# Four small reorderings in a hybrid mLSTM, HGRN2 and attention encoder block on one core

## The reference, cut to what matters

```
z = RMSNorm(x); proj = z @ w_in
y_m = mLSTM branch: 4 heads x 256, chunks of 128, forward and backward
y_h = HGRN2 branch: 8 heads x 128, forward and backward
x = x + (sig(gate_m) * (y_m @ w_branch_m) + sig(gate_h) * (y_h @ w_branch_h)) @ w_out
u = RMSNorm(x, norm_x_g); mn = RMSNorm(mem, norm_mem_g)
probs = softmax((u @ w_q)(mn @ w_k)^T / 16)      # 4 heads x 256, 256 memory tokens
x = x + (probs @ (mn @ w_v)) @ w_o
x = x + ConvGatedFFN(RMSNorm(x)); out = RMSNorm(x)
```

## Time and profile before

| | |
|---|---|
| median of 3 runs | 2550.45 us (2549.9 to 2551.49) |
| profiled execution, its own time | 2551.23 us |
| span of the profiled execution | 2549.5 us |
| mean granted TensorE clock | 0.999 of full speed |
| TensorE busy | 2527.5 us, 99% |
| VectorE busy | 1636.8 us, 64% |
| ScalarE busy | 914.8 us, 36% |
| GpSimd busy | 745.4 us, 29% |

### The profile page before, as it was taken

The page is one execution under the profiler, slowest core; times in us unless marked ns, Lnnn a source line. Parts: engine busy times, 40 slices in busy tenths (PEclk is TensorE's granted clock), DMA queues, the critical chain, the costliest instruction groups (busy, mean ns, idle before and its releaser), DMA issues.

```text
span 2549.5 us, 33564 instructions
## 1 busy us (share of the span) xinstructions
PE 2527.5 (99%) x13158; PEld 2157.2 (85%) x13158; DVE 1636.8 (64%) x1864; ACT 914.8 (36%) x1122; POOL 745.4 (29%) x713
## 2 busy tenths in 40 slices
PE   9999999999999999999999999999999999999998
PEld 9888888889999999997888888876788888888887
DVE  6675555248888888866555424433457998887567
ACT  6342222133333333332323423333333443333433
POOL 2032232002121121234442001177413456553001
PEclk9999999999999999999999999999999999999999
DMA  8323333432223323344443536156414233225755
GB/s 294 121 96 108 99 127 105 140 140 92 84 100 108 107 93 116 108 150 140 165 149 145 201 125 215 34 192 208 155 49 149 85 114 131 101 99 194 276 191 182
DMA packets 181628, 349.67 MB, mean 137 GB/s; under 512 B 10459, under 2 KB 106023, under 8 KB 181472
## 3 DMA queue, kind: packets, MB, share of 16 engines
q1 hardware_dynamic: 119520, 154.44, 18.3%
q0 software_dynamic: 33088, 118.51, 13.3%
q10 hardware_dynamic: 28864, 74.59, 8.0%
HBM read 241.16 MB, written 106.33 MB: 136 GB/s over the span
## 4 chain that ended last, share of the span: by engine, by line
PE 96%; DMA 2%; DVE 1%; ACT 0%; issue 0%; POOL 0%; SPq 0%; ACTq 0%; DVEq 0%; POOLq 0%
PE ps L2301 18%; PE ps L2851 13%; PE ps L2440 12%; PE ps L2869 8%; PE ps L2332 7%; PE ps L2681 7%; PE ps L2507 4%; PE ps L2819 3%; PE ps L2464 3%; PE ps L2590 3%; PE ps L2611 2%; PE ps L2629 2%; PE ps L2379 2%; PE ps L2534 2%; PE ps L2522 1%; PE ps L2792 1%
## 5 line engine op out<-in xcount | busy, mean ns | idle before, releaser
L2301 PE MATMUL ps<-a_hi,whi 128*128 128x512 f32 x576 | 234.2, 407 | 0.0
L2301 PE MATMUL ps<-a_hi,wlo 128*128 128x512 f32 x576 | 224.8, 390 | 0.0
L2301 PE MATMUL ps<-a_lo,whi 128*128 128x512 f32 x576 | 224.4, 390 | 0.0
L1620 DVE TENSOR_TENSOR wlo<-raw,whi 128x2048 fp32r<-128x2048 f32 x59 | 135.8, 2302 | 114.4 <-ACT whi L997 113.3
L997 ACT ACTIVATE whi<-raw 128x2048 fp32r<-128x2048 f32 x59 | 113.1, 1917 | 190.4 <-PE ps L2681 105.1
L1002 ACT ACTIVATE ev<-ps 128x512 f32<-128x512 f32 x128 | 76.6, 599 | 208.0 <-PE ps L2301 131.2
L2332 PE MATMUL ps<-whi,a_hi 128*128 128x256 f32 x512 | 148.1, 289 | 0.0
L2332 PE MATMUL ps<-whi,a_lo 128*128 128x256 f32 x512 | 144.8, 283 | 0.0
L2332 PE MATMUL ps<-wlo,a_hi 128*128 128x256 f32 x512 | 144.7, 283 | 0.0
L793 POOL TENSOR_TENSOR cv<-cv,cs 128x1024 f32<-128x1024 f32 x16 | 38.5, 2404 | 322.6 <-ACT cs L1261 322.6
L2301 PEld LDWEIGHTS ps<-a_hi,wlo 128*128 128x128 f32 x576 | 108.1, 188 | 23.5
(11 more groups left out here) (422 smaller groups left out, 7197.1 us busy)
## 6 DMA issues: line engine op xcount, KB each, us to landing
raw<-in_w_in SPq DMA_DIRECT2D x45, 1024.0 KB, 6.6
raw<-in_w_up SPq DMA_DIRECT2D x22, 1024.0 KB, 5.1
hg_T<-ev ACTq DMA_DIRECT2D x32, 512.0 KB, 3.0
qfb<-hg_T POOLq DMA_DIRECT2D x24, 512.0 KB, 5.5
wd<-in_w_down POOLq DMA_DIRECT2D x44, 256.0 KB, 3.4
down_weight_sums<-wd POOLq DMA_DIRECT2D x22, 512.0 KB, 4.3
hidden_T<-ga ACTq DMA_DIRECT2D x11, 1024.0 KB, 4.0
hidden_sums<-s POOLq DMA_DIRECT2D x10, 1024.0 KB, 4.7
```

The lines of the kernel that those rows point to most:

```text
L1620: signal(dve, dve.tensor_tensor(wlo[:, b.slot], w4[:, b.slot], whi[:, b.slot], ALU.subtract), w_lo, b.count())
L2301: ins = pe.matmul(ps[:, unit_bank(b, u)], W[sw][:, b.slot, k, c * P:(c + 1) * P], op[mw][:, k, t * HALF:(t + 1) * HALF], start=k == 0 and ...
```

## The change

Four edits:

1. SyncE's first loads: the identity and the gain row of the memory norm are issued before the second memory tile, and the first x tile before weight block 1.
2. First mLSTM head (`step` is 0 there): 2 quarters in place of 3 ahead of the scores, one quarter in each of the eight steps (before, none in steps 0, 1 and 7), and after the second head's scores 2 and 1 in place of 3 and 2. The total stays 16.
3. VectorE makes `y_lo` in the iteration of step 6 in place of after step 7.
4. Attention: the reciprocal and multiplication of tile t follow the maximum of tile t, after a wait for its exponential.

```diff
             rows_in(0)
+            sp.dma_start(ident[:], A["c_ident"]).then_inc(id_ld, 16)
+            sp.dma_start(nb["gb"][:, 0], A["norm_mem_g"].to_broadcast([P, D])).then_inc(g_ld, 16)
             rows_in(1)
-            sp.dma_start(nb["gb"][:, 0], A["norm_mem_g"].to_broadcast([P, D])).then_inc(g_ld, 16)
-            sp.dma_start(ident[:], A["c_ident"]).then_inc(id_ld, 16)
             kv_weights(0)
+            rows_in(2)
             kv_weights(1)
-            rows_in(2)
...
+                    if s == 6 and last:
+                        dve.wait_ge(y_cut, 2)
+                        signal(dve, dve.tensor_tensor(y_lo[:], mk[:], y_hi[:], ALU.subtract), y_sub, 2)
                 if not last:
                     head_cols(j + 1)
                     split_lo(b.ahead(1))
-                else:
-                    dve.wait_ge(y_cut, 2)
-                    signal(dve, dve.tensor_tensor(y_lo[:], mk[:], y_hi[:], ALU.subtract), y_sub, 2)
...
-                    if t >= 1:
-                        k = (r - 1) % 3
-                        dve.wait_ge(a_exp, r)
-                        line(dve.reciprocal(mx[:, k, 2:3], mx[:, k, 2:3]))
-                        signal(dve, dve.tensor_scalar(pr[:, k], pr[:, k], mx[:, k, 2:3], None, ALU.mult), a_nrm, r)
+                        dve.wait_ge(a_exp, r + 1)
+                        line(dve.reciprocal(mx[:, r % 3, 2:3], mx[:, r % 3, 2:3]))
+                        signal(dve, dve.tensor_scalar(pr[:, r % 3], pr[:, r % 3], mx[:, r % 3, 2:3], None, ALU.mult), a_nrm, r + 1)
...
                 if not step:
                     ml_keys(0)
-                    quarters(3)
+                    quarters(2)
                     ml_scores(0)
                     quarters(1)
...
                     if s == NT - 1:
-                        quarters(2 if last else 1 if step else 0)
+                        quarters(2 if last else 1)
...
-                        quarters(2 if last else 1 if step or s > 1 else 0)
+                        quarters(2 if last else 1)
                 if not last:
                     ml_keys(j + 1)
                     quarters(2)
                     ml_scores(j + 1)
-                    quarters(4 if step else 3)
+                    quarters(4 if step else 2)
                     result_T(j, (2, 6))
-                    quarters(2)
+                    quarters(2 if step else 1)
```

## The result

The change makes the kernel slower. Median of 12 runs 2557.44 us (2554.06 to 2559.02) against 2551.10 us (2549.90 to 2552.67) in 12 runs of the kernel before: ratio 1.0023, 95% interval 1.0015 to 1.0030, that is 6.3 us more (3.8 to 7.7). The forecast was 2549.5 us, its range ended at 2553.5, and slower by over 0.2% had 4%. Direction and size are both wrong. The profiled execution took 2558.65 us with a span of 2556.9, so 7.4 us of span are to be found, 1.1 more than the medians differ by.

What follows compares the result with a forecast made beforehand. TensorE was taken to bound the kernel, busy 2527.5 of 2549.5 us, with 9.4 us of listed waits. Terms +2.5 - 1.1 + 0 - 2.4 = -1.0 us gave a median of 2549.5 us, range 2546.0 to 2553.5.

Steps and rivals of the forecast that it cites:

- Part B: First mLSTM head: earlier scores save time, a wait moves to the second head's step 0; -1.1 us, bounds 0 and -3.5.
- a quarter there is free: First mLSTM head, step 1: VectorE's chain sets the step's length, so an added quarter turns waiting into work at no cost.
- Part A: Loads at the start: the later second memory tile delays GpSimd's chain and the second key-value block; +2.5 us.
- the second memory tile at about 8.7: Start: exchanged with the gain row in the queue, this tile arrives 2.9 us later.
- Rival 4: Start: a 3.1 us wait before the second key-value block halves the clock for that block, 5.8 us more, 2555.3 us; 3%.
- Part C: Kept keys' low part: the 1.2 us branch-product wait goes but returns at later waits, the load chain holding; 0 us.
- the 1.0 us at the result's transposes: Last mLSTM result: transposes, reached 1.2 us earlier, wait 1.0 us for the scaling of Hm after GpSimd's norm.
- Part D: Attention: with maximum and division adjacent, most probability-transpose waits go; 1.7 of 4.1 us stay, so -2.4 us.
- rival 3: Attention, tiles 5 to 7 of head 3: VectorE idles during exponentials, other work queues behind; +1.5 us, 2553.4 us; 12%.

Runs made afterwards that it cites:

- e1_loads: Only the new order of the first loads, on the kernel before: 2554.42 us against 2551.22, ratio 1.0013.
- g3_loads_fill: The new load order and the new quarters of the first mLSTM head together, on the kernel before: 2557.29 us against 2551.21, ratio 1.0024.
- f1_rstd_first: The new load order, plus GpSimd's rstd of tile 2 ahead of its memsets, on the kernel before: 2552.81 us against 2550.85, ratio 1.0010.
- f3_gate_early: The first head's new quarters, plus ScalarE's gate unit copy ahead of the decay exponential, on the kernel before: 2551.36 us against 2550.85, ratio 1.0003.
- e2_fill: Only the new quarters of the first mLSTM head, on the kernel before: 2553.92 us against 2551.22, ratio 1.0010.
- g4_no_loads: The whole change without the new load order, on the kernel before: 2552.41 us against 2551.21, ratio 1.0003.
- f4_fill: Kernel before with other first-head quarters: two before the scores, one in each of steps 1 to 5, three before the second head's scores: 2549.74 us against 2550.85.
- e3_keys: Only the move of VectorE's y_lo to step 6, on the kernel before: 2551.17 us against 2551.22, ratio 0.9998.
- e4_softmax: Only the new attention order, maximum and division of one tile adjacent, on the kernel before: 2549.01 us against 2551.22, ratio 0.9990.
- f2_row_only: Of the new load order only the first x tile ahead of weight block 1, on the kernel before: 2550.62 us against 2550.85, ratio 0.9999.

## Why the prediction was wrong, part by part

In one sentence: the step that failed is Part B's "a quarter there is free"; in its place the runs show 2.1 us of wait behind a ScalarE copy, and falls of the clock of 1.7 us each. Part A's transfer time was too small besides.

**Part A, +2.5.** Right in mechanism, wrong in size, and incomplete. The exchange does delay tile 2's rstd through GpSimd's program order, and in the profile of e1_loads, where the tile came at 9.15, that chain moved by 3.0 us. The term "the second memory tile at about 8.7" was mis-sized: it took it that the gain row, issued ahead of the tile, would land earlier by as much as the tile lands later. It did not. The row landed at 7.5 to 8.6 in the ten profiles with the old order and at 7.7 to 9.0 in the four with the new: it followed the transfer ahead of it by 1.8 to 2.9 us before, and by 3.2 to 4.2 us now. The memory tile came 1.3 us behind it, at 9.1 to 10.3 in place of 5.7 to 5.9. In the profile after it landed at 10.3, and these 1.6 us are nearly all of the difference between 2.5 and 4.3. They are also the late end of a scatter: e1_loads and g3_loads_fill, with tiles at 9.1 and 9.3, have +3.0 and +3.2 at the second block. The sentence that the first block does not move is wrong too: it came 0.5 us late in e1_loads and 2.5 in the profile after (17.54), behind the transposes of tile 1 at a fallen clock. (The 15.00 of before is itself late: the nine other profiles with the old order have 14.0 to 14.7.) f1_rstd_first shows what that second path costs with GpSimd's repaired: 2.0 us.

**Part B, -1.1.** This is the step that turned the sign: "a quarter there is free". I had read only VectorE's chain for the steps and not who releases the PSUM bank that a quarter writes. Four quarters make one gate unit and fill a bank, the units take two banks in turn, and ScalarE's copy L1333 frees a bank. With quarters in steps 0 and 1 and one fewer ahead of the scores, the third unit starts in step 5 and no longer in step 6. It needs the copy of the first one, and that stands in ScalarE's program behind the decay exponential L1214, which waits for VectorE's Em at 1172.40 and pays a table load of 1.28 us. Before, the copy ran at 1173.86 and the quarter that needs it at 1178.02; now TensorE is there first and waits 2.11 us. f3_gate_early removed that order, and with it the wait: 2.1 of the 2.7 us by the profiles, 2.2 by the medians. The second wait, 2.13 us for L1383, was forecast as 2.3, and its mechanism was right to the point: from the last Em product of step 7 to the key products of step 0 of the second head it is 20.02 to 20.06 us in all fourteen profiles, with three different fills and with or without a fall of the clock. The account of the stretch: the forecast's -1.1, 2.1 for the unforeseen wait and 1.7 for each of two falls of the clock make +4.4; measured +4.3. The profiles with one fall in the head measure one fall less: +2.7 in e2_fill, +2.7 in g3_loads_fill, +2.4 in g4_no_loads. f4_fill, without either wait, has -1.4.

**Rival 4, the clock (3%).** Right kind, wrong place and far too small a chance. I looked for a fall only where a wait was said to be 3.1 us, and let the waits of 1.4 us in the trace of before stand for all shorter ones. Waits of 2.1 to 2.4 us lay between and were not bounded: a wait of 2.3 us stood in my own Part B, without a price for what it does to the clock. Nine of the waits of this size in the profiles were followed by a fall (three in the profile after, one each in e1_loads, e2_fill, f3_gate_early and g4_no_loads, two in g3_loads_fill), three were not (e2_fill, g3_loads_fill, g4_no_loads), and none of 1.4 to 1.8 us was. f1_rstd_first is apart: its stretch of 6.8 us lay around two such waits. The Trainium skill (TensorE: Matmul & The Clock Gate, HAM oscillation) takes the extra wall time of throttled stretches as half their length. The runs agree: 3.4 us at a granted clock of 0.50 cost 1.7. It also (same page, Seeing it yourself) says that the clock records of trn2 traces have been seen to be unreliable and wants them cross-checked. Here the durations do that: eight key products take 3.66 us where they took 1.97.

**Part C, 0.** Right in the number: e3_keys gives 0.9998, and the load chain holds. The place of the second wait was right as well (1.42 and 1.73 us at the second branch block, forecast 0.7), but the 1.0 us at the result's transposes is in none of the three profiles with this edit. That term took Hm's scaling as fixed, and it came 1.1 us earlier, since GpSimd's L885 fell from 1.31 to 0.20 us. e3_keys has 0.78 us at the product of the a_raw rows in its place, the change has nothing there. The second block itself comes 0.8 us (e3_keys), 0.4 (g4_no_loads) and 0.2 us (the change) later than the first head's end would have it; the profiles without this edit have -0.4 to +0.4 there.

**Part D, -2.4.** The number is right (-2.4 in the profile, -2.2 by the medians of e4_softmax), its terms are not, so part of it is luck. The stage scatters: against the profile of before it is 2.0 to 4.2 us shorter in the five profiles with this edit and 0.1 to 1.5 us shorter in the eight without. The mean of the five and that of the nine without the edit, the kernel before among them, differ by 2.2 us. The waits left are 3.3 us in the profile after, not 1.7: at the last tile of head 3 1.78 in place of 0.6, at tile 3 0.70 in place of 0.3, because the maximum now stands behind a low part of the attended rows, which was rival 3's mechanism at a smaller place. What made up for it is a gain that I did not see: a tile without a wait is 2.48 us, not 2.66. TensorE's weight loads had waited for pr in 15 places for 10.2 us before, in 6 for 5.7 after, and a tile seems to pay for such a wait even where the matmul shows none: the one tile of head 3 in the profile after whose weight load waits 0.40 us and whose matmul does not (1811.66 to 1814.26) takes 2.60 us.

**Sum.** 4.3 + 4.3 + 0.2 + 1.05 - 2.4 = +7.4 us, the whole difference of the two spans. The forecast was -1.0: 1.8 short in A, 5.4 in B, 0.2 in C, and 1.05 on the way to the output product. That last one is not the change's: e4_softmax, which alters nothing before attention, has +1.0 there, f2_row_only +0.7, e1_loads +0.1. The profile of before was the quickest of all in this stretch, as it was the slowest of the nine without edit 4 in attention.

**Left open.** The four edits alone add up to 3.2 + 2.7 + 0 - 2.2 = 3.7 us, and the whole is 6.3. Each figure has an interval of 2.3 us to each side, so the difference is not shown. A second fall in the head, 1.7 us, which of all profiles only that of the change has, would explain most of it. The mean granted clock of each run, known to 0.001, says that its other runs have it too: on average 0.9970 in the twelve runs of the change, 0.9978 in the eleven of g3_loads_fill and 0.9991 in the kernel before. A fall of 3.4 us lowers the mean by 0.0007, so as an estimate the change has three falls a run and g3_loads_fill two, as their profiles do. Yet the two kernels are the same up to the last head, so edits 3 and 4 can't be what brings the third. Why one wait of 2.1 us brings a fall and the next does not was not tried. Nor was why the gain row lands no earlier when it is issued earlier, or what makes the first wait at the output product (L2679) 0.3 us in the change and 1.6 in g4_no_loads.

## What to carry to other kernels

Before moving filler in front of a wait, list for every piece who frees the buffer that it writes and what stands ahead of that instruction in its own engine's program; idle time on the filled engine says nothing about it. Price a new wait by what the longest wait seen so far did to the clock: where the trace only has waits up to 1.5 us, one of 2.3 is outside its evidence, and each of the head's two, with the fall behind it, cost nearly twice its length in the profile after. A load that moves ahead in a queue can delay the one it passes (here by 3.4 to 4.6 us) without landing earlier itself, and the tile that is passed can carry a longer chain, here through GpSimd's program order, than the one that gains. When an operation of VectorE is moved, look also at what GpSimd does beside it in the old place and in the new.

## What was not expected of the hardware

The gain row, 4 KB spread over 128 partitions, took 1.8 to 2.9 us behind the memory tile and 3.2 to 4.2 us behind the identity, and landed no earlier for it. GpSimd's L885 took 1.31 us beside a VectorE subtraction and 0.20 us alone. The granted clock fell to half in stretches of 3.4 us after waits of 2.1 to 2.4 us, in a kernel whose TensorE is busy for 99% of the span, and in f1_rstd_first it stayed there from 11.3 to 18.2 us.
